# An attention loop in which VectorE scales the older unit before it masks the next

## What is computed

```python
for l in range(DEPTH_2):                       # 2 layers
    o_a = swa_mixer(...)                       # sliding window 128, 8 heads, with a sink
    o_b = nsa_mixer(...)                       # compressed, selected and window branches, gated
    o_c = mla_mixer(...)                       # latent attention, causal
    ...
    x = x + cross_attn(...)                    # 4 heads of 128 over 256 memory tokens
```

## Time and profile before

| | |
|---|---|
| median of 2 runs | 3372.14 us (3365.02 and 3379.25) |
| the profiled execution | 3364.28 us, of it 3362.5 span |
| TensorE busy | 3248.0 us, 97% of the span |
| VectorE busy | 1470.0 us, 44% |
| ScalarE busy | 680.1 us, 20% |
| granted TensorE clock, mean | 0.991 of full speed |

### The profile page before, as it was taken

One profiled execution on the slowest core, in us unless ns is written; L12 is line 12 of the kernel. 1 busy time (PEld: TensorE's weight loads), 2 busy tenths in 40 slices (PEclk: granted clock), 3 DMA queues, 4 the chain that ended last, 5 costly groups with the idle time before them and its releaser, 6 DMA issues.

```text
span 3362.5 us, 36976 instructions
## 1 busy us (share of the span) xinstructions
PE 3248.0 (97%) x14532; PEld 2077.9 (62%) x14532; DVE 1470.0 (44%) x2922; ACT 680.1 (20%) x1418; POOL 148.8 (4%) x106
## 2 busy tenths in 40 slices
PE   8999999999999999999999999999999999999998
PEld 3445345433433575755866888848467478578887
DVE  2352114212113747736634544355584475254533
ACT  2132020000003425313021000032451331210000
POOL 3400010000000000000000000000000000000000
PEclk9999998999999999999999999999999999999999
DMA  6020725999996121120222222212202112222221
GB/s 243 32 81 32 263 100 198 409 409 409 408 409 238 44 94 39 39 81 26 88 75 75 87 90 91 94 50 88 75 8 88 50 65 99 69 77 80 91 91 69
DMA packets 118636, 433.43 MB, mean 129 GB/s; under 512 B 13120, under 2 KB 13888, under 8 KB 117696
## 3 DMA queue, kind: packets, MB, share of 16 engines
q1 hardware_dynamic: 114768, 417.91, 33.4%
q10 hardware_dynamic: 3696, 13.16, 1.0%
HBM read 427.87 MB, written 3.15 MB: 128 GB/s over the span
## 4 chain that ended last, share of the span: by engine, by line
PE 85%; DVE 6%; DMA 4%; ACT 2%; issue 1%; DVEq 1%; POOL 0%; ACTq 0%; SPq 0%
PE bank L622 83%; DMA arena<-in_stream 2%; DMA ring<-in_stream 2%; PE bank L1218 2%; DVE arena L2215 1%; DVE arena L2240 1%; DVE arena L2237 0%; DVEq L2214 0%; DVE arena L2265 0%; DVE bank L2206 0%; DVE bank L2202 0%; ACT arena L1558 0%; ACT arena L1630 0%; DVE arena L2051 0%; ACT arena L1595 0%
## 5 line engine op out<-in xcount | busy, mean ns | idle before, releaser
L622 PE MATMUL bank<-arena 128*128 128x256 f32 (+14 forms) x5448 | 937.3, 382 | 35.9 <-issue 9.6
L622 PEld LDWEIGHTS bank<-arena 128*128 128x128 f32 (+4 forms) x5448 | 597.2, 169 | 334.6 <-issue 207.2
L622 PE MATMUL bank<-h,ring 128*128 128x256 f32 (+1 forms) x2000 | 668.5, 486 | 3.0 <-ACT rstd L1641 1.7
L622 PEld LDWEIGHTS bank<-h,ring 128*128 128x128 f32 x2000 | 377.4, 190 | 255.0 <-issue 224.0
L622 PE MATMUL bank<-arena,ring 128*128 128x256 f32 (+2 forms) x1888 | 514.3, 426 | 5.0 <-DVE y L1920 3.5
L622 PEld LDWEIGHTS bank<-arena,ring 128*128 128x128 f32 (+1 forms) x1888 | 336.2, 186 | 166.7 <-issue 122.3
L622 PE MATMUL bank<-ring,arena 128*64 128x512 f32 (+2 forms) x1184 | 285.4, 610 | 21.1 <-ACT arena L1441 11.6
L622 PE MATMUL bank<-y,ring 128*128 128x256 f32 (+1 forms) x800 | 253.9, 473 | 1.5 <-DVE y L2001 1.5
L622 PE MATMUL bank<-y,arena 128*128 128x256 f32 (+1 forms) x1032 | 231.8, 381 | 0.0
L1779 POOL TENSOR_TENSOR sq<-sq 128x512 f32<-128x512 f32 (+1 forms) x62 | 78.9, 1273 | 3145.4 <-ACT sq L1422 3145.4
L622 PEld LDWEIGHTS bank<-ring,arena 128*64 128x64 f32 (+2 forms) x1184 | 91.2, 140 | 203.3 <-issue 163.0
(11 more groups left out here) (302 smaller groups left out, 2513.6 us busy)
## 6 DMA issues: line engine op xcount, KB each, us to landing
ring<-in_stream SPq DMA_DIRECT2D x629, 512.0 KB, 4.6
arena<-in_stream SPq DMA_DIRECT2D x168, 512.0 KB, 12.6
x<-in_xT ACTq DMA_DIRECT2D x1, 2048.0 KB, 11.2
arena<-in_memT ACTq DMA_DIRECT2D x2, 1024.0 KB, 6.9
outT<-h ACTq DMA_DIRECT2D x8, 256.0 KB, 2.2
arena<-in_ctxT ACTq DMA_DIRECT2D x1, 1024.0 KB, 5.4
y<-in_inv ACTq DMA_DIRECT2D x1, 1024.0 KB, 4.9
memory_kv<-arena ACTq DMA_DIRECT2D x1, 1024.0 KB, 3.9
```

The costliest lines, as they stand in the source:

```text
L622: ins = pe.matmul(out, lhsT, rhs, start=start, stop=stop, skip_group_check=loose)
```

## The change

In VectorE's loop the block that scales unit s-1 is moved, unchanged, ahead of the block that masks unit s. `between(s)` stays last.

```diff
                     for s in range(len(us) + 1):
+                        if s >= 1:
+                            u = us[s - 1]
+                            n = ub + u["n"]
+                            dve.wait_ge(exped, n + 1)
+                            if u["kind"] == "cmp":
...
+                            else:
+                                told(dve.reciprocal(rden[:, n % 4, 0:2], den[:, n % 4, 0:2]))
+                                for side in range(2):
...
+                                ins.then_inc(scaled, 1)
                         if s < len(us):
                             u = us[s]
                             n, nk = ub + u["n"], u["nk"]
...
                                 dve.tensor_reduce(nbias[:, n % 4, 0:2], S[:, :, 0:w], AX.X, ALU.max, negate=True
                                                   ).then_inc(biased, 1)
-                        if s >= 1:
-                            u = us[s - 1]
-                            n = ub + u["n"]
-                            dve.wait_ge(exped, n + 1)
...
-                                ins.then_inc(scaled, 1)
                         if between is not None:
                             between(s)
```

More of the change, by code:

```diff
@@ L2178, in attend @@
                     for s in range(len(us) + 1):
+                        if s >= 1:
[3 more added lines that the diff above has]
+                            if u["kind"] == "cmp":
+                                p4 = probs[:, n % 3, :, 0:4 * CB].rearrange("p g (t c) -> p g t c", t=4)
+                                r8 = rden[:, n % 4, :].rearrange("p (g t) -> p g t", g=2)
+                                told(dve.tensor_reduce(den[:, n % 4, :].rearrange("p (g t) -> p g t", g=2), p4, AX.X, ALU.add))
+                                told(dve.reciprocal(rden[:, n % 4, :], den[:, n % 4, :]))
+                                told(dve.tensor_tensor(rden[:, n % 4, :], rden[:, n % 4, :],
+                                                       sgate[:, u["qt"], :].rearrange("p (h b) -> p h b", b=3)[:, :, 0],
+                                                       ALU.mult))
+                                dve.tensor_tensor(p4, p4, r8.rearrange("p g (t c) -> p g t c", c=1)
+                                                  .to_broadcast([P, 2, 4, CB]), ALU.mult).then_inc(scaled, 1)
+                            else:
+                                told(dve.reciprocal(rden[:, n % 4, 0:2], den[:, n % 4, 0:2]))
+                                for side in range(2):
+                                    p = probs[:, n % 3, side, 0:u["nk"]]
+                                    r = rden[:, n % 4, side:side + 1]
+                                    if u["gate"] is None:
+                                        ins = dve.tensor_scalar(p, p, r, None, ALU.mult)
+                                    else:
+                                        g = u["gate"][side]
+                                        ins = dve.tensor_scalar(p, p, r, sgate[:, u["qt"], g:g + 1], ALU.mult, ALU.mult)
+                                ins.then_inc(scaled, 1)
                         if s < len(us):
```

## The result

The changed kernel took 3462.57 us (median of two runs, 3458.82 and 3466.33), against 3372.14 before: 1.026 times as long, 95% interval 1.0218 to 1.0301. The profiled execution after took 3466.33 us, with a span of 3464.5. A second set of runs of the same kernel gave 1.0233 (1.0206 to 1.0260). The change makes the kernel slower by 2.3 to 2.6%, on the forecast's side and inside its range, 23 us above the forecast.

What follows compares the result with a forecast made beforehand. TensorE's step was taken to bound 512-key units, VectorE almost as long; at 128 keys TensorE waits for scaling. Sections' 53 + 5 + 2 + 7 = 67, with half-clock ends +68, gave 3432 profiled, median 3440; range 3412 to 3474 us.

Steps and rivals of the forecast that it cites:

- The ring: Attention: mask, exponentials and scaling run one after another, 4.35 us a turn at 512 keys, was 3.07; 3440 us, chance 0.76.
- Section 1, +26.5 per layer: Section 1, 36 units per layer: 123.7 us from first mask to last transposes against 97.2, +53 in two layers.
- already given back: Section 1, last b tile: the old 4.10 us stall before a score matmul goes, as masks precede the helpers.
- Section 0, +3.5 and +1.5: Section 0, 16 units: turns total 50.2 us against 46.7 in layer 1 and 48.7 in layer 2.
- section 0 nearly unchanged: Sign expected in the timeline after: section 0 keeps nearly its old length, while section 1 takes about 124 us.
- second claim: Section 0, value-tile steps: scaling first lets the transposes before a value tile start about 1 us sooner.
- Section 2, +2 and 0: Section 2, from the fourth mask on: 41.5 us against 39.4 in layer 1; nothing left to lose in layer 2.
- Section 3, +3.5: Section 3, 8 units per layer: 20.3 us against 16.8, +7 in two layers.
- 1 or 2 us for a section that ends at half clock: Section ends: allowance for TensorE at half clock, added to the 67 us of the sections to make +68.
- (B): Ring closes and the clock falls for long in section 1: 15 us per layer plus 10 at ends, 3480; chance 0.14.
- (C): Exponentials stay covered; only 128-key and section 3 units lengthen, +10 to +25, 3390; chance 0.07.
- (D): Faster: earlier scaling removes waits in section 1 and before value tiles, at best 2 x 10 us, 3352; chance 0.03.

Runs made afterwards that it cites:

- padded pair: One extra single-column ScalarE copy after each unit's exponentials, in the old order and in the new; against the kernel before: 0.9978 (old order), 1.0304 (new order).
- the split: New order with scaling split by side: VectorE scales the first side while ScalarE does the second exponential; ratio 1.0152 to the kernel before.
- doubled scores: Each unit's scores computed twice in most steps of sections 0 to 2, in both orders; against the kernel before: 1.0176 (old order), 1.0358 (new order).
- the repeat: The changed kernel run again with no edit, against the kernel before: 3451.34 us (5 runs), ratio 1.0233.
- mixed orders: Old order with scaling first in chosen steps of sections 0 to 2 and a b-tile helper moved (0.9982), or in four section 0 steps only (1.0000).
- filled steps: New order with scores computed three times or twice in late steps of sections 0 to 2 where TensorE is thin; ratio 1.0230 to the kernel before.
- section-alone kernels: New order in section 1 alone, or in all other sections alone, old order elsewhere; against the kernel before: 1.0181 and 1.0053.

## Why the prediction was right, and where its size was off

**The ring.** Right, as a mechanism and within 0.01 us a turn. The turns summed from rows of the kernel before were 4.35, 3.74, 3.14, 2.53, 3.34 and 2.52; measured were 4.35, 3.74, 3.13, 2.52, 3.34 and 2.51. The compressed unit, put at 3.1 between bounds of 2.5 and 4.35, was 3.11; that was luck, since it was set beside the 256-key unit by its columns and not summed. What made the rest possible is that every part of a turn stood in the old trace, though never one behind another. The padded pair shows that the exponential's length is paid in each turn of the new order alone, the split shows that only what lies outside it counts, and the doubled scores show that TensorE doesn't limit the turn in section 1.

**Section 1, +26.5 per layer; measured +30.8 and +30.9.** The turns gave the forecast; 4.3 us were missing. In layer 1, 2.0 is the pair of turns after the last b tile and 2.3 the end of the section; in layer 2 the turns are 2.7 longer (0.7 of it at full clock) and the end 1.6. Here a sentence of the prediction failed: it said that the old stall of 4.10 us before a score matmul "is already given back". The stall stayed, at 5.24 us, since the helper that TensorE waits for is issued behind the maximum of step 5, and step 5 comes later by the longer turns ahead of it (this reason is read from the code and the timeline; no run moved that helper in the new order). Behind it the clock fell, on exactly the two instructions that the ring waits for.

**Section 0, +3.5 and +1.5; measured +7.1 and +3.7.** The ring's total again holds (turns 3.34 and 2.46). The end costs 2.25 us more than allowed in each layer, and in layer 1 one value-tile turn, behind a stretch at half clock, 1.4, which the repeat didn't show. So the sign "section 0 nearly unchanged" failed in layer 1. The prediction's second claim, that scaling first lets a value tile's transposes start earlier, is right where the ring isn't closed: the mixed orders gain 1.5 us per layer by it.

**Section 2, +2 and 0; measured +4.4 and +1.3. Section 3, +3.5; measured +3.4.** As forecast, but for the ends of section 2.

**The clock.** The direction was right: by far the most of the time at half clock lies inside the ring and costs nothing. The term of the sum was mis-sized: "1 or 2 us for a section that ends at half clock" should have been about 17, from 12 at six section ends (7.5 of them given back in the four that the filled steps cured), 4 behind the b tile and 1.4 in one value-tile turn. The prediction had the bound in hand, "up to 3 us each, six ends", and put it in no term, although every section end of the new order has the thin TensorE of the earlier trace rows. With that bound in the sum the forecast would have been about 3456.

The page on the clock that the prediction weighed (the Trainium skill, "TensorE: Matmul & The Clock Gate", section "A second HAM failure mode: psum-queue depth-cycling") describes, for another kernel, swings between the two levels where TensorE pauses briefly between groups of matmuls, and throughput lost by them. The trace agrees on the swings, 13.7 us at half clock before and 92.2 after. On the loss it agrees only where somebody waits for TensorE: 17 us of 86. The rest of the slowdown is the ring, at whatever clock: the padded, split and section-alone kernels move with its turns.

**The rivals.** (B), the clock falling for long inside section 1 at 1.2 us per unit, is out: turns with 256 to 512 keys stayed at the full-clock sum, but for two per layer behind the b tile and two in layer 2 that are 0.35 longer. (C) is out: masks are 4.35 apart, not 3.07. (D) decides only in section 0's value-tile steps, where it is real, with 3 us in all of the 20 that it was given at best, and only while the ring is open elsewhere.

## What to carry to other kernels

Where one engine does the step before and the step after another engine's work, the order "older unit's second step, then newer unit's first step" closes a ring, even though it sounds like doing the more urgent work first; "newer unit's first step, then older unit's second" keeps a unit in flight. Its cost can be summed from the old trace: add the parts of one turn, hand-overs included, and compare with the step as it is, for each size by itself. Idle time of the engine that isn't the bottleneck is then the first row to read after the change, and for every thin stretch that the change makes, look for work on TensorE that somebody waits for at its end, and price that at the half-clock duration.

## What the runs showed of the hardware that was not expected

TensorE with *more* to do was faster at the end of a section: with scores computed two or three times, the merge's first eight matmuls took 1.99 us at four of six ends, where they had taken 3.12 to 3.78, and the stretch from the first maximum is 9.6 us shorter in that trace (the medians don't show it). It doesn't always work: with 17.14 us busy of 24 the clock was 0.95 over the 128-key part of section 1, layer 1, and still fell right behind it, for the eight matmuls that matter.

The 16 us ahead of attention are a stretch at half clock of 37.5 us near 266 us of the span, with TensorE busy throughout. Windows of the same place, the kernel before and then the kernel after:

```profile
268.00:300.00 32.00, 31.77 (x175) 21.93 (x176) 7.33 (x24) 10.93 (x13) 0.00 (x0) 1.00 0.06 17
```

```profile
268.00:300.00 32.00, 32.00 (x105) 23.23 (x106) 3.68 (x13) 7.68 (x8) 0.00 (x0) 0.50 0.00 1
```

Of the thirteen profiled executions, six don't have it (the kernel before, the padded pair, the two one-part kernels, the split one), six do (the new order twice, the two mixed ones, the filled one, the old order with doubled scores), and the new order with doubled scores has a shorter one; no edit changes what these programs do before 1100 us. What brings it on is open. It is worth a fifth of the whole effect here, and goes with the spread of the runs of one kernel (3360.86 to 3385.91 for the kernel before on one chip): a difference of 10 us between two single profiles of this kernel says nothing until the place of it is known.
